# Moving the split of transposed hidden tiles, four banks for a small down product, and one weight half ahead of sums, in a two-layer hybrid encoder

## The reference, cut to what matters

```python
def _swiglu(x, w_up, w_down):
    a, b = jnp.split(x @ w_up, 2, axis=-1)
    return (jax.nn.silu(a) * b) @ w_down
x = x + 0.5 * _swiglu(_rms_norm(x, ffn1_norm[i]), ffn1_w_up[i], ffn1_w_down[i])
```

## Time and profile before

| what | value |
|---|---|
| median of 3 runs | 2915.93 us (2915.36 to 2924.39) |
| the profiled execution's own time | 2905.7 us |
| its span, first to last instruction | 2904.0 us |
| mean granted TensorE clock | 0.992 of full |
| busy share: TensorE / VectorE / ScalarE / GpSimd | 96 / 76 / 51 / 5% |

### The profile page before, as it was taken

One profiled execution on the slowest core, in us unless ns is written; L12 is line 12 of the kernel. 1 busy time (PEld: TensorE's weight loads), 2 busy tenths in 40 slices (PEclk: granted clock), 3 DMA queues, 4 the chain that ended last, 5 costly groups with the idle time before them and its releaser, 6 DMA issues.

```text
span 2904.0 us, 33994 instructions
## 1 busy us (share of the span) xinstructions
PE 2800.7 (96%) x12782; PEld 2268.0 (78%) x12782; DVE 2211.4 (76%) x2788; ACT 1492.0 (51%) x2074; POOL 140.1 (5%) x237
## 2 busy tenths in 40 slices
PE   7899999999999999999999999999999999999998
PEld 6777787777778887777777777877777788877777
DVE  8666679999996567666776666889999866776664
ACT  5444456767754435334453344666776634444443
POOL 1000001110001000000000000110110010000000
PEclk9999999999999999999999999999999999999999
DMA  6433224333336343223332232333333463323321
GB/s 195 120 105 95 58 80 107 106 102 97 104 103 192 94 145 102 87 88 87 115 103 87 87 87 73 90 99 90 103 105 98 114 184 95 131 87 92 98 72 66
DMA packets 367018, 300.74 MB, mean 104 GB/s; under 512 B 16863, under 2 KB 313703, under 8 KB 366855
## 3 DMA queue, kind: packets, MB, share of 16 engines
q1 hardware_dynamic: 346848, 260.08, 30.9%
q0 software_dynamic: 17296, 37.29, 4.3%
q10 hardware_dynamic: 2711, 1.21, 0.2%
HBM read 278.97 MB, written 19.53 MB: 103 GB/s over the span
## 4 chain that ended last, share of the span: by engine, by line
PE 94%; DVE 3%; issue 2%; ACT 1%; ACTq 0%; DMA 0%; DVEq 0%
PE bank L1635 43%; PE bank L1711 28%; PE bank L1811 16%; PE bank L1932 2%; PE bank L1746 1%; DVE blk L1119 1%; PE bank L1976 1%; ACT whi L652 1%; PE bank L1984 0%; PE bank L1910 0%; PE bank L1898 0%; PE bank L2011 0%; DVE CA L1306 0%; PE bank L1916 0%; DMA dtbA<-in_ssd_A_log 0%
## 5 line engine op out<-in xcount | busy, mean ns | idle before, releaser
L1109 DVE TENSOR_TENSOR wlo<-blk,whi 128x1024 fp32r<-128x1024 f32 x280 | 342.3, 1223 | 182.6 <-ACT whi L652 180.7
L652 ACT ACTIVATE whi<-blk 128x1024 fp32r<-128x1024 f32 x280 | 295.6, 1057 | 352.6 <-PE bank L1811 267.4
L1109 DVE TENSOR_TENSOR wlo<-wraw,whi 128x1024 fp32r<-128x1024 f32 x328 | 399.2, 1220 | 98.9 <-ACT whi L652 98.6
L652 ACT ACTIVATE whi<-wraw 128x1024 fp32r<-128x1024 f32 x328 | 345.8, 1058 | 241.5 <-PE bank L1635 96.5
L1635 PE MATMUL bank<-uhi,whi 128*128 128x512 f32 x896 | 357.3, 399 | 0.0
L1635 PE MATMUL bank<-hhi,whi 128*128 128x512 f32 x896 | 357.3, 399 | 0.0
L1635 PE MATMUL bank<-hlo,whi 128*128 128x512 f32 x896 | 349.1, 390 | 0.0
L1635 PE MATMUL bank<-ulo,whi 128*128 128x512 f32 x896 | 349.1, 390 | 0.0
L1635 PE MATMUL bank<-uhi,wlo 128*128 128x512 f32 x896 | 348.9, 389 | 0.0
L1635 PE MATMUL bank<-hhi,wlo 128*128 128x512 f32 x896 | 348.9, 389 | 0.0
L1437 DVE SCALAR_TENSOR_TENSOR cacc<-vp,cwg,cacc 128x512 f32<-128x512 f32 x464 | 321.5, 744 | 0.0
(11 more groups left out here) (276 smaller groups left out, 4893.9 us busy)
## 6 DMA issues: line engine op xcount, KB each, us to landing
blk<-in_ffn_w_up SPq DMA_DIRECT2D x160, 512.0 KB, 4.1
wraw<-in_w_in SPq DMA_DIRECT2D x160, 512.0 KB, 4.0
wraw<-in_ffn_w_down SPq DMA_DIRECT2D x88, 512.0 KB, 4.7
wraw<-in_ssd_w_out SPq DMA_DIRECT2D x32, 512.0 KB, 4.3
wraw<-in_ffn_w_up SPq DMA_DIRECT2D x16, 512.0 KB, 3.6
y_spill<-yz POOLq DMA_DIRECT2D x16, 512.0 KB, 3.2
yraw<-y_spill POOLq DMA_DIRECT2D x32, 256.0 KB, 3.9
wraw<-in_conf_w_out SPq DMA_DIRECT2D x16, 512.0 KB, 4.8
```

What stands on the lines that cost most here:

```text
L652: a_.activation(whi[:, t % RING, :], raw_of(t), ACT.Copy).then_inc(hi_ready, 1)
L1109: v_.tensor_tensor(wlo[:, t % RING, :], raw_of(t), f32(whi[:, t % RING, :]), ALU.subtract).then_inc(lo_ready, 1)
```

## The change

There are three edits.

1. `turned_back(n)` replaces the splitting inside the events. For g above 0, tiles 0 and 1 are split together at the start of product 1's steps, ahead of `high_part` and `low_part` of that product, and tiles 2 and 3 at the start of product 2's. For g = 0 the two tiles are turned after product 2 instead of product 0, and split at the start of product 3's steps.
2. The small down part uses four banks, 6, 7 and the pair that group 0 calls Y. Output m waits for output m-4; outputs 2 and 3 wait for VectorE's last additions from the Y pair (`c_ready`).
3. At the very start VectorE makes the low half of slab 3 (`low_part(S + 3)`) before the first three sets of `s_sums` instead of after them.

```diff
+        def d_bank(f, part, m):
+            return (6, 7, *PAIRS[f][2])[m % 4] if part == 0 else 6 + m % 2
...
+                    def turned_back(n):
+                        if n in (1, 2) and g:
+                            for j in range(2 * n - 2, 2 * n):
+                                h_high(L, f, 4 * g - 2 + j, h[0], j, T_BANKS[j])
+                        if n == 3 and not g:
+                            for j in range(2):
+                                h_high(L, f, j, h[0], j, T_BANKS[j])
...
-                        if n == 1 and (g or t < 2):
-                            h_high(L, f, 2 + 4 * (g - 1) + t if g else t, h[0], t, T_BANKS[t])
...
-                            if g:
-                                h_high(L, f, 4 * g + t, h[0], 2 + t, T_BANKS[2 + t])
...
                     for n in range(PRODUCTS):
+                        turned_back(n)
                         high_part(b + 2 * n + 3)
                         event(n, 0)
...
                     low_part(AHEAD - 1)
+                low_part(S + 3)
+                if N == 0:
                     dve.wait_ge(prm_ps, 2 * DEPTH)
                     for i in range(3):
                         s_sums(0, i)
-                low_part(S + 3)
...
-                            v_.scalar_tensor_tensor(out=xf[:, m, :], in0=bank[6 + m % 2][:, :], scalar=0.5,
+                            v_.scalar_tensor_tensor(out=xf[:, m, :], in0=bank[d_bank(f, part, m)][:, :], scalar=0.5,
...
                     product(0, X, True)
-                    for j in range(2):
-                        turn(g - 1 if g else None, j, T_BANKS[j])
+                    if g:
+                        for j in range(2):
+                            turn(g - 1, j, T_BANKS[j])
...
                     product(2, Y, True)
+                    if not g:
+                        for j in range(2):
+                            turn(None, j, T_BANKS[j])
...
-                        if m >= 2:
-                            pe.wait_ge(x_done, xb + part * KD + m - 1)
+                        if part == 0 and m in (2, 3):
+                            pe.wait_ge(c_ready, FI * FG * 6 + 3 + m)
+                        held = 2 if part else 4
+                        if m >= held:
+                            pe.wait_ge(x_done, xb + part * KD + m - held + 1)
```

More of the change, by code:

```diff
@@ L792, in up @@
                     X, Z, Y = (pairs[(g + i) % 3] for i in range(3))
+                    def turned_back(n):
[5 more added lines that the diff above has]
+                                h_high(L, f, j, h[0], j, T_BANKS[j])
                     def event(n, t):
+                        if n in (1, 5):
+                            return
                         if t == 0:
@@ L1299, in piece, with turned_back @@
                                                 op0=ALU.mult, op1=ALU.mult).then_inc(h_ready, 1)
+                    def turned_back(n):
+                        if n in (1, 2) and g:
+                            for j in range(2 * n - 2, 2 * n):
+                                h_low(L, f, 4 * g - 2 + j, h, 0, j, T_BANKS[j])
+                        if n == 3 and not g:
+                            for j in range(2):
+                                h_low(L, f, j, h, 0, j, T_BANKS[j])
                     def event(n, t):
@@ L1306, in event @@
                             v_.tensor_tensor(CA[:, t, :], bank[Z[t]][:, :], CA[:, t, :], ALU.add).then_inc(c_ready, 1)
[L1307 to L1310, removed]
                         if n == 4:
@@ L1820, in down @@
                             pe.wait_ge(lo_ready, S + d + j + 1 + RING)
-                        if m >= 2:
-                            pe.wait_ge(x_done, xb + part * KD + m - 1)
+                        if part == 0 and m in (2, 3):
[3 more added lines that the diff above has]
+                            pe.wait_ge(x_done, xb + part * KD + m - held + 1)
                         for k in range(nk):
-                            ins = feature_major(bank[6 + m % 2][:, :], (S + d + j) % RING, (k * each + mm) * P,
+                            ins = feature_major(bank[d_bank(f, part, m)][:, :], (S + d + j) % RING, (k * each + mm) * P,
                                                 H[0][:, k, :], H[0][:, 4 + k, :], k == 0, k == nk - 1)
```

## The result

The changed kernel takes 2821.03 us, median of 4 runs (2819.77 to 2826.05), against 2915.88 for the kernel before in 4 runs of the same chip. The ratio is 0.9671, interval 0.965 to 0.9693: 3.3% faster. The forecast was 2831, range 2816 to 2858. The profiled execution took 2820.6 us against 2905.7, where the sum had given 2820.9.

A forecast was written before the change was run, and what follows sets the result against it. TensorE, busy 2800.7 of 2904.0 us, was taken to bound the kernel. Gains of 57.6 + 26.6 + 0.6 = 84.8 us gave 2820.9 profiled and 2915.93 - 84.8 = 2831.1 us timed, range 2816 to 2858.

The forecast's parts named there:

- the weight-load side: At the 16 turn gaps, TensorE's idle time read at weight loads: 52.8 us, against 49.4 on the matmul side.
- the 4.8 us of clock in the groups 1: Group 1 of three feed-forward parts ran longer at lower clock after the 3.09 us gap; 4.8 us would return.
- The spare time at the second slab of product 3: Tightest slab after the turned tiles move: low half ready at 194.3, needed at 196.8, 2.5 us to spare.
- weights become late: Rival, chance 0.08: product 3's second slab comes 1 us too late in each group, 16 us come back, 2847.
- the turn still waits: Rival, chance 0.03: tile 1's low half is not in front after all, 16 x 3.3 us stay, 2884.
- slower: Rival, chance 0.01: ScalarE's high halves wait behind the transposes; ending slower needs 5.3 us given back per group.
- the clock drops in the gaps that stay: Rival, chance 0.05: after 1.00 us gaps the four small down parts run slower, 9 us in all, 2840.
- keep its length: Rival, chance 0.05: four banks only shift the small down part's wait to later outputs, gaining nothing, 2858.
- 3.72 - 2.72 = 1.00 us stays: Small down part: outputs 2 and 3 fill 2.72 of the 3.72 us gap; output 4 still waits 1.00.
- 0.1 for the restart: Small down part: allowance after the remaining gap, in 10.88 + 1.00 + 0.1 = 12.0 us per part.
- The charge for the clock behind it: Product 0, behind the moved start gap: 2.3 us lost to lower clock, as after the old gap.
- the 10.2: Whole kernel: timed median's excess in us over the profiled time, carried over unchanged to reach 2831.1.

The follow-up runs named there:

- add_first: Changed kernel, with VectorE adding outputs 0 and 1 of the small down part before the slab's low half: 2816.83 us, ratio 0.9679.
- banks_only: Kernel before with only the four banks in the small down part: 2885.89 us, ratio 0.9914.
- no_low: Changed kernel without the early low half of slab 3 at the start: 2821.57 us, ratio 0.9696.
- turned_only: Kernel before with only the reordered turned tiles: 2849.67 us, ratio 0.9788.
- low_only: Kernel before with only slab 3's low half made ahead of the first sums: 2914.11 us, ratio 1.0002.
- after_again: The changed kernel, unaltered, run again in a later comparison: 2822.91 us, ratio 0.9694.
- both: Changed kernel with outputs 0 and 1 added first and VectorE's parameter copies moved into product 5 of group 0: 2816.83 us, ratio 0.9672.
- tail_kept: Changed kernel with the turns of g = 0 back in product 1, one tile for each CA event: 2825.13 us, ratio 0.9707.

## Why the prediction was right, and where it was off

**Edit 1: right in place, mechanism and size.** 16 groups are 64.95 - 61.66 = 3.29 us shorter, 52.6 in all against 52.8 forecast; the weight-load side of the earlier trace rows was the right one to take, not the 49.4 of the matmul side. The 4.8 us of clock in the groups 1 came back as well: 57.4 against 57.6. The spare time at the second slab of product 3 was 2.6 us (2.5 forecast), although one more sum stands behind that slab, at 183.19, where the prediction had none left. So the rival *weights become late* had no ground, and neither had *the turn still waits* and *slower*.

**Edit 2: right mechanism, one term mis-sized.** The gap at output 4 is 1.09 (1.00 forecast), and the clock stayed at 1.00 through all four parts, against the rival *the clock drops in the gaps that stay*; nor did the part *keep its length*. But each part took 12.41 instead of 12.0. The term that was too small is "3.72 - 2.72 = 1.00 us stays" with "0.1 for the restart". It was read on the matmul side, while edit 1 had been read on the weight-load side. On that side the gaps are these: the waits before, the last matmul ahead of the gap in the kernel after, and the weight load behind it.

```profile
PEld bank L1811 <- DVE xf L1343: 24.0, 8, 4.1
```

```profile
97.48 0.39 PE L1833 MATMUL bank<-hhi,wlo 128*128 128x512 f32 x1
98.93 0.30 PEld L1833 LDWEIGHTS bank<-hhi,whi 128*128 128x128 f32 x2 [1.49 <-issue]
```

The longest wait before was 4.1 and not 3.72. 4.1 - 2.72 gives 1.4, and 10.88 + 1.4 + 0.1 would have been 12.4. The matmul side leaves out two pieces. The 24 matmuls ahead of the gap start at full pace, the last at 97.48 = 92.27 + 23 x 0.2267, but that last one is counted as 0.39 long, 0.16 more than the pace. The 24 behind the gap took 5.72 where 5.44 is usual, 0.28 more. Together 0.44, and `add_first`, with no gap and 10.88, bears it out. The gain is 74.65 - 49.66 = 25.0 instead of 26.6; `banks_only` gave the same 25.

**Edit 3: too small for timed runs, 0.6 forecast.** The gap moved and is 4.87 us long. The charge for the clock behind it was low: 72 matmuls took 19.16 at 0.86, so 2.8 us were lost instead of 2.3. Measured from VectorE's low half of slab 2, product 3 starts after 39.12 us before and 39.08 after, 39.69 in `no_low` and 39.33 in `turned_only`. Over all profiles with the parameter copies in place, the five without edit 3 have 39.12 to 39.69, mean 39.46, and the seven with it 38.10 to 39.21, mean 38.65: 0.8 on average, of the forecast's size, but one pair of profiles can't show it.

**The median: the step that failed.** The edits gave 82.2 us in the profiled pair, where the sum had 84.8; 2.9 by chance in the mixer made up the rest, so it is luck that the profiled time, 2820.6, came within 0.3 of the forecast's 2820.9. The timed median was forecast 10 us higher, 2831.1, by carrying over an excess "with a cause that I can't read from the trace". That step failed: its cause is mostly the clock behind the 3.1 us gaps, and edit 1 removes it with them. In `turned_only` edit 1 is worth (1 - 0.9788) x 2911.55 = 61.7 us in timed runs (56 to 67 by the interval) and 56.1 in the profiled pair, so about 5.6 of the 10.2 are its own (0 to 11 by the same interval); the rest was the draw of the first runs of before. The earlier trace rows gave a hint: 3 of 16 gaps dropped the clock at a cost of 1.6 each, and 5.6 / 1.6 is three or four more of them. The prediction even says that the 4.8 us could be larger in a timed run, and still carried the 10.2 over. The table by clock, the long stretches in `low_only` and `banks_only`, and `turned_only`, whose runs lie at its profiled time, show it. The runs of `turned_only`, which keep the small down parts' gaps, lie within 2.6 us; those of `banks_only`, which keep the turns' gaps, spread over 9.4. That each single longer run had so many long stretches is argued, since only profiled executions have a trace.

**What stays open.** One run of the kernel after (2826.05) and two of `after_again` (2828.84 and its profiled execution, 2830.64 at clock 0.994) are about 5 us or more above the rest. Of the 10 us that the profiled one has more than that of the kernel after, 5.7 are lost in the first mixer and 4.3 in the second, with one wait of 2.7 us in each. In the first TensorE waits for a load, and the granted clock is 0.95 in the 13 us around it:

```profile
PE bank L1935 <- DMA LB<-l_image: 2.7, 1, 2.7
```

The profiles of `no_low` (2.7), `both` (3.0) and `tail_kept` (2.5) have a wait at this place too, without a releaser named. What makes that load late in some executions was not tested, nor how much of the scatter of the kernel before comes from it.

## What to carry to other kernels

When a timed median lies above the profiled execution, look at the mean granted clock of every run before carrying the difference over: here it fell as the time rose, the difference hung on the gaps, and the edit that closed them closed it too. Read a gap on the weight-load side too: here its removal gave back about what that side showed, 3.29 us for 3.30 at the turn and 1.53 for 1.49 in the small down part, where the matmul side showed 3.09 and 1.09. A repeated gap is worth removing whole; shortened from 3.1 to 2.5 us it still cost clock. And before buying buffers for a consumer that comes late, look at what stands ahead of it in its queue: here the two additions placed first took about half of the waits without any bank, and with the banks all of them.

## What the runs showed that I had not expected

- Gaps of 2.50 us in a TensorE otherwise at full clock still dropped it, after 5 of 16, by 1.1 to 1.6 us in the four stretches measured; gaps of 1.09 never did in the kernel after.
- A gap of 1.09 us for the addition of a bank cost 1.53 us in all at a granted clock of 1.00: 0.16 for the end of the last matmul ahead of it and 0.28 for a slower restart.
- With the same 16 gaps of 3.09 us, 3 stretches were slow in the profiled execution of the kernel before (2905.7 us) and 7 in that of `low_only` (2915.9). The slow stretches are 6.3 of those 10.2 us.
